# Six weight chunks behind each layer norm run on centred x, with mean and norm applied when the bank is read

## The reference

```
alpha = (2.0 * DEPTH) ** 0.25            # DEPTH = 2
for l in range(DEPTH):
    x = layer_norm(alpha * x + 0.5 * swiglu_2(x, w_ff1_in[l], w_ff1_out[l]), ln1_g[l], ln1_b[l])
    mix = hybrid_mixer(x, w_in[l], b_in[l], ...)      # one big input projection, three branches, w_out
    x = layer_norm(alpha * x + mix, ln2_g[l], ln2_b[l])
    x = layer_norm(alpha * x + 0.5 * swiglu_2(x, w_ff2_in[l], w_ff2_out[l]), ln3_g[l], ln3_b[l])

def layer_norm(x, g, b):
    mu = jnp.mean(x, -1, keepdims=True); xc = x - mu
    return xc * lax.rsqrt(jnp.mean(xc * xc, -1, keepdims=True) + LN_EPS) * g + b

def swiglu_2(x, w_in, w_out):            # w_in is 1024 x 8192, w_out 4096 x 1024
    gate, up = jnp.split(x @ w_in, 2, axis=-1)
    return (jax.nn.silu(gate) * up) @ w_out
```

## Time and profile before

| what | value |
|---|---|
| three runs | 2614.66, 2618.08, 2621.85 us; median 2618.08 |
| profiled execution | 2620.07 us, of which the span from first to last instruction is 2618.1 |
| TensorE busy | 94% of the span |
| VectorE, ScalarE, GpSimd busy | 68%, 49%, 7% |
| mean granted TensorE clock | 0.964 of full |

### The profile page before, as it was taken

One profiled execution on the slowest core, in us unless ns is written; L12 is line 12 of the kernel. 1 busy time (PEld: TensorE's weight loads), 2 busy tenths in 40 slices (PEclk: granted clock), 3 DMA queues, 4 the chain that ended last, 5 costly groups with the idle time before them and its releaser, 6 DMA issues.

```text
span 2618.1 us, 38249 instructions
## 1 busy us (share of the span) xinstructions
PE 2460.2 (94%) x15544; PEld 2217.3 (85%) x15544; DVE 1788.6 (68%) x2533; ACT 1272.3 (49%) x1895; POOL 182.7 (7%) x180
## 2 busy tenths in 40 slices
PE   7789999979999999988998999999999889989998
PEld 7678889878888887977997888788889879978887
DVE  4769757559858866566457886688665665668865
ACT  4545454545445544465344554454444653545543
POOL 0002000002100001040002000100001300020000
PEclk8899999999999999999998999999999899989999
DMA  5236565425556555522243656466654323436652
GB/s 180 83 123 211 182 211 179 136 91 194 182 175 205 185 185 173 176 97 89 91 152 122 203 190 185 145 206 188 186 178 157 98 89 97 145 112 202 186 176 97
DMA packets 114878, 409.87 MB, mean 157 GB/s; under 512 B 13072, under 2 KB 14992, under 8 KB 114704
## 3 DMA queue, kind: packets, MB, share of 16 engines
q1 hardware_dynamic: 114704, 407.43, 48.6%
HBM read 406.33 MB, written 1.05 MB: 156 GB/s over the span
## 4 chain that ended last, share of the span: by engine, by line
PE 84%; DVE 10%; ACT 4%; issue 1%; DMA 0%; SPq 0%; DVEq 0%; ACTq 0%
PE ps L330 84%; DVE wlo L1479 3%; ACT whi L911 1%; ACT region L1024 1%; DVE x L1599 0%; DVE R L1608 0%; DVE region L2060 0%; DVE x L1613 0%; PE ps L494 0%; DVE region L2063 0%; DMA raw<-in_ew_c 0%; DVE x L1518 0%; DVE xx L1526 0%; DVE region L1707 0%; DVE R L1577 0%
## 5 line engine op out<-in xcount | busy, mean ns | idle before, releaser
L330 PE MATMUL ps<-xx,whi 128*128 128x512 f32 (+1 forms) x5360 | 1494.4, 349 | 65.6 <-DVE xx L1620 16.1
L1479 DVE TENSOR_TENSOR wlo<-raw,whi 128x1024 fp32r<-128x1024 f32 (+2 forms) x772 | 932.8, 1214 | 497.0 <-ACT whi L911 495.9
L330 PE MATMUL ps<-xx,wlo 128*128 128x256 f32 x4056 | 1155.1, 285 | 0.0
L330 PEld LDWEIGHTS ps<-xx,whi 128*128 128x128 f32 x5360 | 954.1, 195 | 200.2 <-issue 29.6
L911 ACT ACTIVATE whi<-raw 128x1024 fp32r<-128x1024 f32 (+2 forms) x772 | 800.2, 1043 | 637.4 <-PE ps L330 637.2
L330 PEld LDWEIGHTS ps<-xx,wlo 128*128 128x128 f32 x4056 | 786.7, 194 | 1.4 <-issue 1.0
L330 PE MATMUL ps<-H,whi 128*128 128x512 f32 (+1 forms) x2144 | 633.0, 358 | 10.0 <-DVE H L1497 10.0
L330 PE MATMUL ps<-H,wlo 128*128 128x256 f32 x1760 | 493.8, 281 | 0.0
L330 PEld LDWEIGHTS ps<-H,whi 128*128 128x128 f32 x2144 | 382.9, 190 | 72.9 <-DVE H L1497 10.7
L330 PEld LDWEIGHTS ps<-H,wlo 128*128 128x128 f32 x1760 | 334.3, 190 | 1.1 <-issue 1.0
L1474 DVE TENSOR_REDUCE t<-ps 128x256 f32<-128x512 f32 x344 | 237.1, 689 | 62.1 <-PE ps L330 51.6
(11 more groups left out here) (251 smaller groups left out, 1306.6 us busy)
## 6 DMA issues: line engine op xcount, KB each, us to landing
raw<-in_sg SPq DMA_DIRECT2D x128, 512.0 KB, 4.1
raw<-in_su SPq DMA_DIRECT2D x128, 512.0 KB, 3.9
raw<-in_sd SPq DMA_DIRECT2D x128, 512.0 KB, 4.3
raw<-in_mw_g SPq DMA_DIRECT2D x48, 512.0 KB, 3.4
raw<-in_fg SPq DMA_DIRECT2D x44, 512.0 KB, 3.3
raw<-in_fu SPq DMA_DIRECT2D x44, 512.0 KB, 3.3
raw<-in_fd SPq DMA_DIRECT2D x32, 512.0 KB, 3.5
raw<-in_mw_a SPq DMA_DIRECT2D x24, 512.0 KB, 3.5
```

The lines of the kernel that those rows point to most:

```text
L330: return e.matmul(out, lhsT, rhs, start=start, stop=stop, skip_group_check=True)
L1479: e.tensor_tensor(m.wlo[:, c % NHL, 0:cw], m.raw[:, c % NRAW, 0:cw], m.whi[:, c % NHL, 0:cw].bitcast(F32), ALU.subtract).then_inc(s["wlo"] ...
```

## The change

Behind five of the six layer norms (not behind end) the first six weight chunks of the next stage no longer multiply the normed x. They multiply x after the early centring and times the gain g, in a new buffer `RX` of two halves, each 258 columns wide: 256 tokens, and g and the bias b of the norm as columns 256 and 257. So a bank holds W(g x), Wg and Wb. When VectorE reads it (`raw`) it copies the two columns, forms mean x Wg - W(g x), and multiplies by the reciprocal root; ScalarE's next operation flips the sign and adds Wb. The first four chunks do their tiles 0 to 6 one chunk after the other, then tile 7 of all four; the matmuls of the norm's statistics stand behind the first chunk (`at=0`) or the second (`at=1`, t0 and t1).

The normed x is still made for all later chunks and the residual: VectorE centres and scales, ScalarE makes the high half and the full x, GpSimd the low half. GpSimd also takes over the running sum of x. The splitting of chunks 4 to 8 moves in the queues: chunk 4 into the norm (ScalarE before it, VectorE behind the reciprocal), chunks 5 and 6 between the tiles k of the norm, 7 and 8 behind it. In the hybrid stage VectorE now reads the first six banks and ScalarE adds the sign and bias to the result. The merged branches are split pair by pair into `mx`, a part of H, with only the last pair behind the last merge. The loads of `rowc`, `relb`, `negd` (and `lvm`) wait for the sixth chunk of the hybrid stage instead of for the first low half, since `RX` lies over their memory.

```diff
# TensorE and memory
+    m.wgb = sb("wgb", [128, 6, 2])
...
+    m.RX = nc.alloc_sbuf_tensor_at("RX", [128, 8, 2, 258], F32R, offset=at + 65536, align_bytes=64)
+    m.mx = m.H[:, 8:16]
...
+    def layer_norm(st):
+
+        w.wait_ge(s["ysum"], st, 6)
+        b = take(6, ("msq", st), ("mean", st))
...
-    def ffn(st, wg, wu, wd, nt, rms, then, ln):
+    def gemm_raw(st, spec, at):
+
+
+
+        def begin(n):
+            name, i, b = spec(n)
+            keys.append((name, i))
+            parts.append((*weights(name, i), b))
+
+        def tile(n, k):
+            wh, wl, b = parts[n]
+            c = k * 128
+            a = m.RX[:, k]
+            return mm3(b[:, 0:258], wh[:, c:c + 128], wl[:, c:c + 128], a[:, 0, :], a[:, 1, :], k == 0, k == 7)
+
+        keys, parts = [], []
+        w.wait_ge(s["rgl"], st)
+        for n in range(4):
+            begin(n)
+            for k in range(7):
+                w.wait_ge(s["rxl"], st, k)
+                tile(n, k)
+            if n == at:
+                layer_norm(st)
+        w.wait_ge(s["rxl"], st, 7)
+        for n in range(4):
+            tile(n, 7).then_inc(s["gemm"].h, s["gemm"].up(*keys[n]))
+        for n in range(4, 6):
+            begin(n)
+            for k in range(8):
+                t = tile(n, k)
+            t.then_inc(s["gemm"].h, s["gemm"].up(*keys[n]))
...
+        if kind == "ln":
+            gemm_raw(st, lambda n: (wu if n % 2 else wg, n // 2, bank(n // 2, n % 2)), at)
+        else:
+            gemm_first(st, [(wu if g else wg, j, bank(j, g)) for j in range(2) for g in range(2)], wide=True)
+        if kind == "rms":
             rms_stats(st)
-        for j in range(2, nt):
-            gemm_wide(wg, j, bank(j, 0))
+        for j in range(3 if kind == "ln" else 2, nt):
+            gemm_wide(wg, j, bank(j, 0), st if kind == "ln" else None)
             gemm_wide(wu, j, bank(j, 1))
...
-        gemm_first(xst, qk)
-        for i in range(4, 8):
-            gemm_fm(f"mw_qkb{l}", i, take(i % 4, ("pact", l, "qk", i))[:, 0:256], xh, xl)
+        gemm_raw(xst, lambda i: (f"mw_qkb{l}", i, take(i, ("rawm", l, i))), 0)
+        for i in range(6, 8):
+            gemm_fm(f"mw_qkb{l}", i, take(i, ("pact", l, "qk", i))[:, 0:256], xh, xl, xst)
...
# ScalarE
             w.wait_ge(s["ycen"] if k < nz else s["xadd"], st, k)
             e.activation(m.t8[k], x[:, k, :], ACT.Square).then_inc(s["xsq"].h, s["xsq"].up(st, k))
+            if st != "end":
+                e.activation(m.RX[:, k, 0, 0:256], x[:, k, :], ACT.Copy, scale=pk(names[0], k)).then_inc(
+                    s["rxh"].h, s["rxh"].up(st, k))
         if n == nz - 1:
             prefetch(ACT.Sqrt)
+            if st != "end":
+                e.activation(m.RX[:, :, 0, 256], pk(names[0], 0, 8), ACT.Copy).then_inc(
+                    s["rgh"].h, s["rgh"].up(st, 0))
+                e.activation(m.RX[:, :, 0, 257], pk(names[1], 0, 8), ACT.Copy).then_inc(s["rgh"].h, s["rgh"].up(st))
...
-    def layer_norm(st, bname, b1, b2, final=False):
+    def layer_norm(st, names):
+        if st != "end":
+            chunk(4)
         w.wait_ge(s["sqsum"], st, 6)
         w.wait_ge(s["stat"], st, "mean")
-        e.activation(m.t8[1], ps[b1][:, 0:256], ACT.Square).then_inc(s["msq"].h, s["msq"].up(st))
+        e.activation(R[:, 0, :], ps[6][:, 0:256], ACT.Copy).then_inc(s["mean"].h, s["mean"].up(st))
+        e.activation(m.t8[1], ps[6][:, 0:256], ACT.Square).then_inc(s["msq"].h, s["msq"].up(st))
         w.wait_ge(s["var"], st)
         e.activation(m.t8[3], m.t8[2], ACT.Sqrt, bias=m.epsc[:, 1:2]).then_inc(s["root"].h, s["root"].up(st))
         for k in range(8):
+            g, b, v = pk(names[0], k), pk(names[1], k), x[:, k, :]
             w.wait_ge(s["xnrm"], st, k)
-            if final:
-                e.activation(x[:, k, :], x[:, k, :], ACT.Identity, bias=pk(bname, k)).then_inc(s["fin"].h, s["fin"].up(k))
-            else:
-                e.activation(xh[:, k, :], x[:, k, :], ACT.Identity, bias=pk(bname, k)).then_inc(
-                    s["xhi"].h, s["xhi"].up(st, k))
-        prefetch(ACT.Silu)
-
-    def ffn(st, wg, wu, wd, nt, rms, tile):
+            if st == "end":
+                e.activation(v, v, ACT.Identity, scale=g, bias=b).then_inc(s["fin"].h, s["fin"].up(k))
+                continue
+            e.activation(xh[:, k, :], v, ACT.Identity, scale=g, bias=b).then_inc(s["xhi"].h, s["xhi"].up(st, k))
+            e.activation(v, v, ACT.Identity, scale=g, bias=b).then_inc(s["xfull"].h, s["xfull"].up(st, k))
+            if k in (3, 5):
+                produce(1)
...
+            if raw(j):
+                if j == 0:
+                    prefetch(ACT.Silu)
+                w.wait_ge(s["rawn"], st, j, 0)
+                e.activation(g, g, ACT.Silu, scale=-1.0, bias=m.wgb[:, 2 * j, 1:2]).then_inc(
+                    s["silu"].h, s["silu"].up(st, j))
...
+            if i < 6:
+                w.wait_ge(s["rawn"], l, i)
+                t = e.activation(dst, dst, ACT.Identity, scale=-1.0, bias=m.wgb[:, i, 1:2])
+            else:
+                w.wait_ge(s["gemm"], f"mw_qkb{l}", i)
+                t = e.activation(dst, ps[i][:, 0:256], ACT.Identity, bias=pk(f"{nm}{l}", i % 4))
+            t.then_inc(s["pact"].h, s["pact"].up(l, "qk", i))
...
# VectorE
+        if st != "end" and n >= nz:
+            for k in range(nz) if n == nz else (n - 1,):
+                raw_low(st, names, k)
...
+        w.wait_ge(s["rxh"], st, k)
+        e.scalar_tensor_tensor(m.RX[:, k, 1, 0:256], x[:, k, :], pk(names[0], k), m.RX[:, k, 0, 0:256].bitcast(F32),
+                               ALU.mult, ALU.subtract).then_inc(s["rxl"].h, s["rxl"].up(st, k))
...
+        w.wait_ge(s["mean"], st)
         centre(0)
         w.wait_ge(s["stat"], st)
-        e.tensor_tensor(m.t8[2], ps[b2][:, 0:256], m.t8[1], ALU.subtract).then_inc(s["var"].h, s["var"].up(st))
+        w.wait_ge(s["msq"], st)
+        e.tensor_tensor(m.t8[2], ps[7][:, 0:256], m.t8[1], ALU.subtract).then_inc(s["var"].h, s["var"].up(st))
         centre(1)
         w.wait_ge(s["root"], st)
         e.reciprocal(R[:, 1, :], m.t8[3]).then_inc(s["rstd"].h, s["rstd"].up(st))
-        for k in range(9):
-            if k < 8:
-                w.wait_ge(s["rstd"], st)
-                w.wait_ge(s["cen"], st, k // 2)
-                e.scalar_tensor_tensor(x[:, k, :], x[:, k, :], pk(gname, k), R[:, 1, :], ALU.mult,
-                                       ALU.mult).then_inc(s["xnrm"].h, s["xnrm"].up(st, k))
+        if st != "end":
+            chunk(4)
+        for k in range(8):
+            w.wait_ge(s["rstd"], st)
+            w.wait_ge(s["cen"], st, k // 2)
+            e.tensor_tensor(x[:, k, :], x[:, k, :], R[:, 1, :], ALU.mult).then_inc(s["xnrm"].h, s["xnrm"].up(st, k))
             if k in (1, 3):
                 centre(k // 2 + 2)
-            if k and not final:
-                j = k - 1
-                w.wait_ge(s["xhi"], st, j)
-                e.scalar_tensor_tensor(xl[:, j, :], x[:, j, :], pk(bname, j), xh[:, j, :].bitcast(F32), ALU.add,
-                                       ALU.subtract).then_inc(s["xlo"].h, s["xlo"].up(st, j))
-
-    def ffn(st, wg, wu, wd, nt, rms, half, tile):
+            if k in (4, 6) and st != "end":
+                produce(1)
...
+    def raw(dst, b, i, key, bias=None):
+
+        w.wait_ge(s["gemm"], *key[0])
+        e.tensor_copy(m.wgb[:, i, 0:1], b[:, 256:257])
+        if bias is None:
+            t = e.tensor_copy(m.wgb[:, i, 1:2], b[:, 257:258])
+        else:
+            t = e.tensor_tensor(m.wgb[:, i, 1:2], b[:, 257:258], bias, ALU.add)
+        t.then_inc(s["wgb"].h, s["wgb"].up(*key[1]))
+        w.wait_ge(s["wgb"], *key[1])
+        e.scalar_tensor_tensor(dst, R[:, 0, :], m.wgb[:, i, 0:1], b[:, 0:256], ALU.mult, ALU.subtract).then_inc(
+            s["rawm"].h, s["rawm"].up(*key[1]))
+        w.wait_ge(s["rawm"], *key[1])
+        e.tensor_tensor(dst, dst, R[:, 1, :], ALU.mult).then_inc(s["rawn"].h, s["rawn"].up(*key[1]))
...
+            if kind == "ln" and j < 3:
+                raw(U, b, 2 * j + 1, ((wu, j), (st, j, 1)))
+                w.wait_ge(s["silu"], st, j)
+                w.wait_ge(s["rawn"], st, j, 1)
+                e.scalar_tensor_tensor(U, U, m.wgb[:, 2 * j + 1, 1:2], G, ALU.subtract, ALU.mult).then_inc(
+                    s["fmul"].h, s["fmul"].up(st, j))
+                return
...
     def hybrid(l):
-        chunk(4)
-        for _ in range(4):
+        for i in range(6):
+            if i >= 4:
+                chunk()
+            dst, nm = (m.qb[:, i, :], "bqb") if i < 4 else (m.kb[:, i - 4, :], "bkb")
+            raw(dst, ps[i], i, ((f"mw_qkb{l}", i), (l, i)), pk(f"{nm}{l}", i % 4))
+        for _ in range(2):
             chunk()
...
+        def split(p):
+            for k in (2 * p, 2 * p + 1):
+                low(m.mx[:, k, 1, :], m.mgs[p][:, k % 2, :], m.mx[:, k, 0, :], ("xhi", "xlo"), f"g{l}", k)
...
# GpSimd
-    def squares(st):
```

(13 more changed lines are left out.)

212 lines of the change are left out of this document (117 added, 95 removed).

## The result

| | before | changed |
|---|---|---|
| median of four runs each, same chip | 2616.37 us (2613.83 to 2621.85) | 2634.89 us (2629.44 to 2639.96) |
| ratio | | 1.0068, 95% interval 1.0040 to 1.0095 |
| profiled execution, its span | 2620.07, 2618.1 us | 2629.44, 2627.6 us |
| VectorE, ScalarE, GpSimd busy | 68%, 49%, 7% | 68%, 50%, 8% |

A forecast was written before the change was run, and what follows sets the result against it. The prediction took TensorE, busy 94% of the span, as the bound. Gains and losses, 2 x 1.1 - 0.8 - 2 x 4.3 + 0.3 = -6.9, took the profiled 2620.07 to 2627.0; forecast 2625 us beside a median of 2618, range 2598 to 2643.

The forecast's parts named there:

- t0 and t1: Layer norms ahead of feed-forward stages, after the merged branches and mw_o; forecast loss 4.3 us each, a 1.25 gain included.
- s01: Layer norm after a last projection, ahead of a feed-forward stage; forecast loss 0.8 us, with 5.4 us idle at chunk 9.
- m0 and m1: Layer norms ahead of the hybrid stages; forecast gain 1.1 us each, with 5.3 us idle ahead of chunk 7.
- the end: Last layer norm: loses a multiplication by g on VectorE, gains a copy of the mean; forecast gain 0.3 us.
- the likeliest case: The forecast itself, 2625 us, its own range 2612 to 2634, chance 0.45.
- The ring: At t0 and t1, ScalarE and VectorE operations in turn for each later tile of RX: 3.8 us a tile against 3.0 before.
- The walk from the mean to chunk 10: At t0 and t1, queues followed as at s01 from the mean at 42.4 us to chunk 10 at 77.3.
- Rival 1: Chunk 9 (7 at m0, m1) within 3 us of its want, clock stays up: 23 us less, 2602; chance 0.25.
- Rival 2: GpSimd's fourteen operations for each norm hold VectorE: 3 us more at each of five norms, 2640; chance 0.22.
- Rival 3: Loads come late at m0 and m1, constants holding the queue 5 us longer: 3 us at each, 2631; chance 0.05.

The follow-up runs named there:

- e5: Changed kernel with each bank read cut to one subtraction, leaving out the two column copies and two products; 2610.85 us.
- e7: The changed kernel run again unaltered, for a second trace; 2633.24 us, ratio 1.0068 (1.0048 to 1.0087) to the kernel before.
- e8: Changed kernel with four re-orderings together: chunks earlier behind all five norms, ScalarE's chunk halves and the statistics earlier at t0, t1; 2611.88 us, ratio 0.9980 to the kernel before.
- e9: Changed kernel with the change undone at t0 and t1 alone; 2617.07 us, ratio 0.9996 (0.9980 to 1.0011) to the kernel before.
- e12: Changed kernel with four re-orderings, the gate banks' reciprocal-root product moved to GpSimd and two column copies made one; 2608.88 us, ratio 0.9974 to the kernel before.
- e6: Changed kernel with GpSimd writing zeros, reading nothing, in place of the low half of the normed x; 2632.35 us.

## Why the prediction was right, and by how much it was off

**The mechanism held, the size did not.** At s01, m0 and m1 TensorE worked through the norm, with waits of 0.8 ahead of chunk 6 and, at s01, 0.9 ahead of chunk 7 (one of 0.9 was forecast), and the pause came where it was put: ahead of chunk 9 with 4.9 to 5.0 us (forecast 5.4) at s01, t0 and t1, ahead of chunk 7 with 4.7 (5.3) at m0 and m1, ended by `wlo`, with the clock at half behind it. `raw` is 1.11 us (1.2). e5 confirms the cause by its size. The norms whose cover succeeded gained nearly nothing, as forecast: 2.3 at m0 and m1 together (2.2), -1.6 at s01 (-0.8), 0.7 at the end (0.3). The two of m0 and m1 fit by luck in part: the prediction took one start for both before, 39.05, where they were 39.89 and 39.15. In all, 7 us of loss were forecast and 18 measured: 2634.9 lies in the wide range, which two rivals had stretched, and just above the likeliest case's own, which ended at 2634.

**The term that was mis-sized is t0 and t1**, 7.0 and 6.1 us instead of 4.3 each. Three parts, in numbers of t0:
- `mw_o` starts 1.56 us behind the branch, not 0.86. A weight chunk's low half stood ahead of the last merge's work on VectorE. The gain against before was 0.55, not 1.25.
- The ring's period was right (3.78 against 3.8 us), but its start was late: the five low halves of `RX` took 3.00 us as one batch with GpSimd's sums beside them (two of the five 0.94, the others 0.48), where I had put 0.4 each, and the weight chunk's low half ahead of them took 1.82 and not 1.22. With the first part, the last tile was released at 37.5 and not at 35.8, and the mean read at 44.0 and not at 42.4: 1.6 us.
- The walk from the mean to chunk 10 is short by 1.1 us, at s01 as well, where all of it is there by chunk 7's low half (done at 24.0, forecast 22.9). ScalarE's sixteen writes of the norm account for it. I took 0.42 each from a row of 507 ns; they now take gain and bias, and the changed kernel shows, by form from 1683 to 1735 us:

```profile
L1052 ACT ACTIVATE xx<-x,pk 128x256 fp32r<-128x256 f32 x8 | 4.7, 593 | 5.6 <-DVE x L1717 5.6
...
L1053 ACT ACTIVATE x<-x,pk 128x256 f32<-128x256 f32 x8 | 4.7, 587 | 0.0
```

Back to back each starts 0.50 us after the one before: 16 times 0.08 is 1.3 us. This is worked out; no run varied these writes alone. The Trainium skill, ScalarE: Activation LUTs, section "What ACT_TABLE_LOAD costs", says that each operand given by a pointer of one value for each partition adds about 93 ns; the rows agree with 86 (593 less 507), and by that rule the term would have been right.

**The sum.** By chunk 10 the five norms and the end lose 11.7 us (11.9 in e7's trace) where 6.9 were forecast. The medians differ by 18, with an interval of 10 to 25 (by 15 in e7, whose ratio says 13 to 23). So 3 to 7 us are not in the norms, and the ratios of e8, e9 and e12 lack 5 to 7 us of what their traces gain there. Most of that is found in the down projections, the last 32 chunks of a feed-forward stage, which read H. Two windows inside the last one, before and changed, both behind chunks of 2.83 us (columns as in the earlier trace rows; the number of matmuls stands behind TensorE's busy time):

```profile
2555.00:2595.00 40.00, 40.00 (x233) 34.99 (x232) 20.99 (x25) 14.82 (x17) 2.94 (x4) 1.00 0.38 124
```

```profile
2565.00:2605.00 40.00, 40.00 (x228) 34.85 (x227) 19.30 (x21) 14.09 (x17) 5.74 (x8) 1.00 0.37 118
```

In the last nineteen chunks of each of the four feed-forward stages of the second block, a chunk took 2.77 us in the trace of the kernel before, whatever the stage's pace until then. It took 2.79 or 2.83 in all four stages of all thirteen traces of the changed kernel and its variants. From chunk 10 to the stage's end, at the same pace of the chunks up to there, t0's stage takes 239.9 us and not 238.9, and t1's 243.5 and not 242.5, in both traces of the changed kernel. That is 1 us for a stage and 4 for the four in these traces, 0.6 at the least in others. The prediction had asked only whether the other engines' extra operations fit beside TensorE's work there, and put TensorE's own work at the same length. What slows it is open: in the changed kernel H lies further on in memory, behind `wgb`, but no run moved it back; and of the kernel before there is one trace.

**The rivals.** Rival 1, the late chunk is not late, fell: no pause was under 4.7 us. The bound I gave for it, a stall of 3.5 us from which the clock falls, was too high: e8's pause of 2.56 at s01 left the clock at 0.50 of full in the next window and a first matmul of 0.77 us. Rival 2, GpSimd holds VectorE, exists but is small at s01: e6 moved chunk 9 by 1.1 us. The prediction read the earlier trace rows as less than a hold to the end of GpSimd's instruction; the timeline under e6 shows that it is one. At t0 GpSimd's sums lengthened three VectorE operations ahead of the mean by 1.5 us together; e6 left them in place, so what they cost there is untested. Rival 3: the constants were issued at 1054.6, 19.3 us behind the last matmul as worked out, and nothing waited for them.

## What to carry to other kernels

Covering a norm with matmuls on raw data removes the wait only if the engines that feed the matmuls have slack for the correction: here VectorE paid 0.5 us more for each of six banks, and 5 us of wait came back at the first chunk that stood behind them. Ask how many chunks later the feeding engine has caught up, and count both ways by which it feeds (its own low halves, and the high halves of an engine that waits for its products): shortening its work pays, re-ordering it moves the wait, and a third engine helps only if its input is not late for the same reason. Where GpSimd works beside VectorE, ask which VectorE operations start while one of its instructions runs: these, and not all, are held to that instruction's end.

## What the runs showed of the hardware that was not expected

TensorE has two paces on the same work at a granted clock of 1.00. In the changed kernel's trace, two windows inside feed-forward stages, ahead of the down projection:

```profile
1760.00:1800.00 40.00, 40.00 (x233) 35.26 (x232) 32.40 (x44) 20.70 (x30) 0.00 (x0) 1.00 0.62 190
2440.00:2480.00 40.00, 40.00 (x228) 34.68 (x228) 31.90 (x43) 20.35 (x30) 0.00 (x0) 1.00 0.60 186
```

And in e7, the same program, two windows of which the second is the first one of above:

```profile
1480.00:1520.00 40.00, 40.00 (x233) 35.33 (x232) 32.57 (x44) 20.79 (x29) 0.00 (x0) 1.00 0.57 187
1760.00:1800.00 40.00, 40.00 (x228) 34.72 (x227) 32.12 (x44) 19.92 (x28) 0.00 (x0) 1.00 0.59 187
```

A chunk of 16 matmuls takes 2.77 or 2.83 us, 2%, some 5 us for a stage. The pace of the chunks that read x holds to the stage's down projection and changes from stage to stage, in the kernel before too (2.77 at t0, 2.83 at s01 and t1), and from run to run of the same program (s01 above). It fits that seventeen runs of the kernel before on one chip lay between 2604.56 and 2627.53. What switches it was not found. The down projection's pace is another matter: it went with the kernel in every trace ("The sum"). The two paces mean that one profile can't tell a difference of 10 us from the span: compare the same event behind the same start instead.

The clock at half after a pause is not tied to one length. Pauses of 4.7 to 5.0 us gave it each time. The same pause of 2.5 us ahead of chunk 7 in e5 was followed by half clock at m0 and not at m1 (chunk 7 took 4.4 and 2.9 us), and the same 2.10 ahead of chunk 12 in e12 by half clock at t1 and not at s01 (4.4 and 2.9 us). It can also come late: e8's 2.56 gave it at s01 from the first matmul on, and at t0 only some matmuls later (first one 0.47 us, then 0.53 of full in the next window).
